# Decay sums spread over the partitions: one fp32 product against two fp32r products

## What is computed

```
g = jnp.cumsum(g, axis=-1)
decay = jnp.exp(jnp.where(tri, g[..., :, None] - g[..., None, :], -jnp.inf))
q_dec = q * jnp.exp(g)[..., None]
```

## Time and profile before

| | |
|---|---|
| median of 3 runs | 1706.6 us (1705.66 to 1709.12) |
| profiled execution, own time | 1714.26 us |
| its span | 1712.5 us |
| TensorE busy | 1648.7 us (96%), 9487 matmul instructions |
| TensorE weight loads busy | 1411.4 us |
| VectorE, ScalarE, GpSimd busy | 850.1, 678.6, 865.5 us |
| mean granted TensorE clock | 0.989 |
| chain that ended last | PE 76%, DVE 15%, ACT 3% |

### The profile page before, as it was taken

One profiled execution on the slowest core, in us unless ns is written; L12 is line 12 of the kernel. 1 busy time (PEld: TensorE's weight loads), 2 busy tenths in 40 slices (PEclk: granted clock), 3 DMA queues, 4 the chain that ended last, 5 costly groups with the idle time before them and its releaser, 6 DMA issues.

```text
span 1712.5 us, 23546 instructions
## 1 busy us (share of the span) xinstructions
PE 1648.7 (96%) x9487; PEld 1411.4 (82%) x9487; DVE 850.1 (50%) x1343; ACT 678.6 (40%) x1010; POOL 865.5 (51%) x485
## 2 busy tenths in 40 slices
PE   7999888999999999999999999999999999999997
PEld 7888878889989888888888878888887778888886
DVE  7778966734443101122111122128999973357744
ACT  5656443242323222233222233333333444366651
POOL 4455534233445545544555555546377466366661
PEclk9999999999999999999999999999999999999999
DMA  5476279464422334333333333332332323333332
GB/s 206 145 249 179 63 199 291 124 187 146 131 82 87 98 99 144 92 96 90 96 98 98 99 99 99 103 107 90 96 97 86 99 86 99 94 96 102 101 101 74
DMA packets 121267, 202.45 MB, mean 118 GB/s; under 512 B 32560, under 2 KB 71624, under 8 KB 121160
## 3 DMA queue, kind: packets, MB, share of 16 engines
q1 hardware_dynamic: 119400, 197.98, 37.8%
q10 hardware_dynamic: 1760, 2.98, 0.5%
HBM read 170.97 MB, written 29.97 MB: 117 GB/s over the span
## 4 chain that ended last, share of the span: by engine, by line
PE 76%; DVE 15%; ACT 3%; issue 2%; DMA 2%; POOL 1%; SPq 1%; DVEq 0%; ACTq 0%; POOLq 0%
PE ps L421 66%; PE ps L1789 4%; DVE ps L1282 4%; DVE cacc L2245 3%; DVE prd L632 2%; DVE inv L635 1%; DVE at L582 1%; DMA d_p<-dec 1%; PE ps L943 1%; PE ps L957 1%; PE ps L964 1%; DVE tmp L2478 1%; PE ps L951 1%; PE ps L968 1%; DVE dec L544 0%
## 5 line engine op out<-in xcount | busy, mean ns | idle before, releaser
L409 POOL TENSOR_TENSOR w_lo<-w_raw,w_hi 128x1024 fp32r<-128x1024 f32 x264 | 632.3, 2403 | 516.3 <-ACT w_hi L403 516.1
L421 PE MATMUL ps<-hp,w_hi 128*128 128x512 f32 (+2 forms) x2432 | 596.6, 345 | 4.8 <-DVE cacc L2245 3.2
L421 PEld LDWEIGHTS ps<-hp,w_hi 128*128 128x128 f32 x2432 | 405.0, 190 | 59.3 <-issue 4.3
L421 PE MATMUL ps<-hp,w_lo 128*128 128x512 f32 (+2 forms) x1216 | 371.7, 343 | 0.0
L403 ACT ACTIVATE w_hi<-w_raw 128x1024 fp32r<-128x1024 f32 x264 | 277.5, 1053 | 158.1 <-DMA w_raw<-in_w 150.2
L421 PEld LDWEIGHTS ps<-hp,w_lo 128*128 128x128 f32 x1216 | 212.3, 190 | 25.9
L421 PE MATMUL ps<-n_hi,w_hi 128*128 128x512 f32 x464 | 183.8, 396 | 2.1 <-POOL w_lo L409 2.1
L421 PE MATMUL ps<-n_hi,w_lo 128*128 128x512 f32 x464 | 180.7, 389 | 0.0
L421 PE MATMUL ps<-n_lo,w_hi 128*128 128x512 f32 x464 | 180.5, 389 | 0.0
L1282 DVE SCALAR_TENSOR_TENSOR ps<-u_in,par,ps 128x511 f32<-128x511 f32 (+14 forms) x240 | 176.7, 739 | 7.5
L421 PEld LDWEIGHTS ps<-n_hi,w_hi 128*128 128x128 f32 x464 | 87.1, 188 | 22.1 <-ACT sg_a L2079 2.5
(11 more groups left out here) (414 smaller groups left out, 2574.8 us busy)
## 6 DMA issues: line engine op xcount, KB each, us to landing
w_raw<-in_w SPq DMA_DIRECT2D x264, 512.0 KB, 3.5
d_y<-zero SPq DMA_DIRECT2D x6, 688.0 KB, 6.0
d_x<-zero SPq DMA_DIRECT2D x6, 688.0 KB, 5.9
d_at<-at SPq DMA_DIRECT2D x16, 256.0 KB, 3.3
d_kc<-kc SPq DMA_DIRECT2D x16, 256.0 KB, 3.3
d_qd<-eg SPq DMA_DIRECT2D x16, 256.0 KB, 3.2
d_p<-dec SPq DMA_DIRECT2D x16, 256.0 KB, 3.3
AT<-d_at SPq DMA_DIRECT2D x16, 256.0 KB, 6.0
```

Source lines behind the costliest of these rows:

```text
L409: e.tensor_tensor(w_lo[:, u % RAW, :], w_raw[:, u % RAW, :], w_hi[:, u % RAW, :].bitcast(F32), ALU.subtract).then_inc(s_lo, 1)
L421: mm = e.matmul(ov, w, r[:, k, t0:t1], start=(first and n == 0 and p3 == 0), stop=(last and n == len(tiles) - 1 and p3 == 2))
```

## The change

The triangles are rounded once to fp32r tiles (`uf_r`, `ub_r`), `gdec` is split into a rounded part `gd_hi` (ScalarE) and a remainder `gd_lo` (VectorE), and each fp32 product of `pe_pg` becomes two fp32r products that accumulate in the same place in PSUM. The first call waits for `gd_lo` as well. The new tiles, 1664 bytes a partition, are put ahead of the region `z0`, which moves up by that, in steps of 256 bytes. The products of `dk` (L1551, L1552) and of the meta tokens (L776) stay fp32.

```diff
+        uf_r, ub_r = put("uf_r", [P, P], F32R), put("ub_r", [P, P], F32R)
+        gd_hi, gd_lo = put("gd_hi", [P, NB, 2 * H], F32R), put("gd_lo", [P, NB, 2 * H], F32R)
...
-        ga = Signal(sem("s_ga"), wba=1, sig=1, eA=1, ex=1, dk=3, lam=1)
+        ga = Signal(sem("s_ga"), wba=1, sig=1, eA=1, ex=1, gh=1, dk=3, lam=1)
...
-        dg = Signal(sem("s_dg"), halo=9, n2=1, zero=1, wlo=1, b=1, ch=20, lam=18, g2=2)
+        dg = Signal(sem("s_dg"), halo=9, n2=1, zero=1, wlo=1, b=1, ch=20, gl=1, lam=18, g2=2)
...
@@ pe_pg
             for d in range(2):
                 if x == 0:
                     e.wait_ge(*ga.at("dk", 3))
+                    e.wait_ge(*dg.at("gl", 1))
...
                 for u in range(HG):
-                    g = gdec[:, c, d * H + h0 + u:d * H + h0 + u + 1].to_broadcast([P, P])
-                    mm = e.matmul(bankv(6 + d, P, P)[:, u], g, cmat("ub" if d else "uf"), start=True, stop=True)
+                    for g in (gd_hi, gd_lo):
+                        mm = e.matmul(bankv(6 + d, P, P)[:, u], g[:, c, d * H + h0 + u:d * H + h0 + u + 1].to_broadcast([P, P]),
+                                      (ub_r if d else uf_r)[:], start=g is gd_hi, stop=g is gd_lo)
                 mm.then_inc(m_gr.sem, 1)
...
@@ act_program
             e.activation(ident_r[:], cmat("ident"), ACT.Copy)
+            e.activation(uf_r[:], cmat("uf"), ACT.Copy)
+            e.activation(ub_r[:], cmat("ub"), ACT.Copy)
...
                     if task == "dk":
+                        e.wait_ge(*dg.at("ch", 20))
+                        e.activation(gd_hi[:], gdec[:], ACT.Copy).then_inc(ga.sem, 1)
                         e.wait_ge(*pg.at("dk", 1))
...
@@ dve_program
+                    if task == "dk":
+                        e.wait_ge(*ga.at("gh", 1))
+                        e.tensor_tensor(gd_lo[:], gdec[:], gd_hi[:].bitcast(F32), ALU.subtract).then_inc(dg.sem, 1)
```

## The result

| | median | lowest to highest | executions |
|---|---|---|---|
| before | 1705.41 us | 1702.78 to 1715.03 | 20 |
| after | 1713.73 us | 1702.08 to 1718.42 | 20 |

The ratio is 1.0038, with a 95% interval from 1.0025 to 1.0051: the changed kernel is slower by about 6.5 us (the ratio is that of the means; the medians are 8.3 us apart). The forecast was "within 0.2%", 1707.0 us with a range of 1702 to 1712; the median lies outside of both, 1.7 us above the range.

The account below looks back on a forecast made before the run. TensorE was taken as the bound, busy 1648.7 of 1712.5 us; its distances add 0.5 us, 0.4 on the path, other work and addresses nothing: 1706.6 + 0.4 = 1707.0 us, range 1702 to 1712 us.

Parts of the forecast that it names:

- the distance: Time between weight loads in pe_pg's calls: 112 ns, bound by the load; estimate near 116 ns, +0.5 us of TensorE.
- ScalarE's slack ahead of tile 7: ScalarE's idle time before tile 7's tap: 0.51 us, with 0.3 us left after gd_hi's added 0.21 us.
- Rivals 1, 2 and 4: In pe_pg's calls: 1, streaming binds, 1702.4 us, 8%; 2, slow narrow products, 1715.1 us, 6%; 4, 256 instructions, 1717 us, 2%.
- rival 2: In pe_pg's calls, narrow fp32r products stream as four passes: distance 213 ns, 102 ns more; 1715.1 us; chance 6%.
- the sum: Whole kernel: median 1706.6 us plus 0.4 us gives 1707.0 us; difference within 0.2% (3.4 us).
- Rival 3: Around pe_pg's calls, shorter streaming lets the clock fall more often: two falls more, +5 us, 1711.6 us; chance 8%.

Follow-up runs that it names:

- e1: The kernel before with the four new tiles allocated but unused, so only addresses move: 1705.34 us, ratio 0.9996.
- e2: The changed kernel with the 64 fp32 products back; tiles, copies, split and waits stay: 1704.97 us, ratio 0.9988 to before.
- e10: The changed kernel with only the fourth pe_pg call streaming 256 columns in three of four heads: 1706.09 us, ratio 1.0004 to before.
- e3: The changed kernel again, word for word, to trace a usual execution: 1714.6 us, ratio 1.0046 to before; profiled execution 1713.39 us.
- e4: The changed kernel with GpSimd's remainder of weight units 17 to 25 in four pieces of 256 columns: 1706.1 us, ratio 0.9998 to before.
- e8: The changed kernel with GpSimd waiting, in tiles 16 to 22, for VectorE's first tap: 1705.3 us, ratio 0.9995 to before.
- e7: The kernel before with GpSimd waiting, in tiles 16 to 22, for VectorE's first tap: 1706.2 us, ratio 0.9996.
- e11: The kernel before with 46 useless 268-column products on TensorE ahead of tile 17's product: 1704.87 us, ratio 0.9997.

## Why the prediction was wrong

**Right, by its own steps.** The trace has 128 instructions; the distance is 112 to 113 ns as before (taken: 112, estimate 116) though the passes are halved, so they give nothing. The copies last 0.30, `gd_hi` 0.25 and `gd_lo` 0.24 us, all hidden; ScalarE's slack ahead of tile 7 is 0.17 us (predicted 0.3), VectorE's 5.33 us (5.4). Addresses cost nothing (e1), nor do copies and waits (e2). Rivals 1, 2 and 4 are refuted. The rate of 0.42 ns a column from which the prediction works out its times of streaming (2.4 columns a nanosecond in rival 2) is that of rows 2: the fp32r forms last 287 ns at 268 columns and 389 ns at 512, 102 ns for 244 columns. At 512 columns an fp32 instruction lasts 598 ns, 209 ns more than the fp32r one; streaming 512 columns once more takes 214 ns at that rate, so it streams them twice. One statement is a little off without bearing on the forecast: rival 2's distance is 101 ns more, not 102.

**Wrong in size.** I expected 230 ns for a narrow fp32r instruction. In the trace's rows for L521 it is 274 ns, as in the fp32 form:

```profile
L521 PE MATMUL ps<-uf_r,gd_hi x32: 222/274/454, 78.0 to 263.0; 128*128 128x128 f32 x32
...
  DVE dec L548: 2.2, 3
```

(Minimum, median and maximum in ns, and VectorE's wait for these products, 2.2 us in three waits instead of the predicted near 4.2.) So the duration of a 128-column instruction does not tell how often it streams while the distance is set by something else. That it streams once shows where one stands behind a 256-column instruction, in e10's fourth call:

```profile
136.41 0.22 PE L522 MATMUL ps<-ub_r,gd_hi 128*128 128x128 f32 x1
136.47 0.27 PE L522 MATMUL ps<-ub_r,gd_lo 128*128 128x128 f32 x1
```

It lasts 0.22 us, as predicted, and the next one starts 60 ns after it; two passes of 128 columns would need 107 ns at 0.42 ns a column.

**The step that failed** is the sum, which put everything outside of `pe_pg` and task `dk` at nothing: "The difference from before lies within 0.2% (3.4 us)". It added up what changed on the path of the change's own engines, and took the rest of the kernel as fixed: "The forecast is wrong if [...] anything outside `pe_pg` and task `dk` moved". Nothing was moved there, but the times of tiles 17 to 22 depend on which engine comes first, and the change tipped that. Rival 3 had the mechanism by which it was tipped, less streaming and a fall of the clock where none came. It had three things wrong:
- The place. It counted "five calls in places with idle time" without naming them, priced them by the chunk loop and looked for "a lower mean clock between 225 and 300 us". There before has 0.95, e3's long execution 0.95 as well, and after's short one 0.93. The fall that matters is behind the fourth call, at 136 us.
- The price. It gave a fall "1.5 us here, plus as much again for its neighbours" (for two falls this is 6 us, not the 5 of its sum). The fall itself costs less than this: tile 16's taps start 1.2 us later, and e4's and e8's profiled executions have the fall and are short all the same (1702.8 and 1704.13 us). The loss comes with the absence of the fall at 159 us and with the six collisions that follow; the spans of the two profiled executions differ by 8.7 us.
- The chance. It was given 8%, with two falls needed; in e3 one did it. 22 of 26 executions of the changed kernel are long; how many of these had the fall only their traces would tell, and only one of them, e3's, has a trace.

The numbers fit: the share of long executions rose from 10 of 103 to 22 of 26, by 0.75; 0.75 x 8.7 us = 6.5 us, which is the measured difference of the means.

There was also a reading to be had beforehand. The profiled execution of before was 7.7 us above the median, and the prediction noted this and went on. Its timeline had six chain instructions of 2.4 to 2.5 us beside others of 0.20 to 0.60 us, and the chain that ended last ran through them. An execution so far off the median with an instruction six times its usual length suggests that the kernel has two courses, and that a change ahead of tile 17 may choose between them.

**Left open.** Why a single kernel now takes one course and now the other; before's own long execution had neither fall, so the fall at 136 us is one way into the collided course and not the only one. That the clock is the link between the columns of the fourth call and the course is read from one profiled execution of each kernel; no run held the clock up at 136 us by other work. Nor does a run show why the later fall stays away after the earlier one, beyond the idle stretch that is 2.38 instead of 2.84 us. The clock also falls between 84 and 94 us (mean 0.83) in eight of the thirteen profiled executions, among them after's (clear) and e3's (collided); so it goes with neither course. No version here beats both kernels: e2, e7, e8 and e11 all have before's time.

## What to carry to other kernels

- Before saving matmul passes in narrow products, look at the distance between weight loads: here, at 128 columns and 128 weight columns, 112 to 113 ns went by in either form, so half the streaming was worth nothing, and its loss behind an idle stretch of 1.3 us went with a fall of the clock (0.76 from 134 to 141 us in e3, 1.00 in e10).
- If the profiled execution is well off the median, look first at what differs in it, an instruction several times as long as its like above all; a profile from the rarer group shows another kernel than the one that is timed.
- A shift of a microsecond or two can decide whether two engines meet in every turn of a loop. Before adding up only what a change does on its own path, look for such meetings in the stages behind it.
- Where a GpSimd pass over SBUF and a VectorE chain with two SBUF operands share a loop, look whether they meet: here an instruction of the chain took 2.45 us beside the pass instead of 0.36, and the taps, which read PSUM, 3.18 us with it and without. One wait tied the GpSimd pass to the taps, and made both kernels' times narrow (1703.23 to 1707.52 us and 1701.74 to 1708.23 us).

## What the runs showed of the hardware

- Four GpSimd instructions back to back held up one VectorE instruction throughout, 3.16 us (e4); it did not get in between the pieces, where others of the same execution did, in 0.66 to 0.83 us.
- A fall of the clock was worth more than it cost, by the lateness that it brought: with the clock kept up by 20 useless products the kernel took 1715.68 us, before beside it 1705.46 us, and with 46 such products, late and at the full clock, 1704.87 us.
- In two calls of the same 16 weight loads, both starting at 134.70 us and as long to 0.02 us, the clock fell behind the one that streamed 128 columns in each instruction (e3) and not behind the one with 256 in twelve of the sixteen (e10).
- Weights that are fp32r loaded no faster than fp32 ones: the median is 192 ns for `gd_hi` in the changed kernel and 190 ns for the fp32 loads of L518 before, and a call's 16 loads take 1.88 and 1.87 us.
